# The copy of the transposed product in the delta-rule inverse: from ScalarE to VectorE

## The reference, cut to what matters

```python
m = jnp.where(strict, beta[..., :, None] * kk * decay, 0.0)
a = m + jnp.eye(C, dtype=f32)
...
sol = lax.linalg.triangular_solve(a, rhs, left_side=True, lower=True, unit_diagonal=True)
u, w = sol[..., :DV], sol[..., DV:]
```

## Time and profile before

| | |
|---|---|
| median of 3 runs | 2104.67 us (2101.84 to 2105.86) |
| the profiled execution | 2100.9 us |
| its span, first to last instruction | 2099.0 us |
| granted TensorE clock, mean | 0.961 of full speed |
| TensorE busy | 1930.8 us, 92% |
| VectorE busy | 1279.5 us, 61% |
| ScalarE busy | 984.5 us, 47% |
| the chain that ended last, by engine | PE 85%, DVE 7%, ACT 5%, issue 1%, DMA 1% |

### The profile page before, as it was taken

One profiled execution on the slowest core, in us unless ns is written; L12 is line 12 of the kernel. 1 busy time (PEld: TensorE's weight loads), 2 busy tenths in 40 slices (PEclk: granted clock), 3 DMA queues, 4 the chain that ended last, 5 costly groups with the idle time before them and its releaser, 6 DMA issues.

```text
span 2099.0 us, 27446 instructions
## 1 busy us (share of the span) xinstructions
PE 1930.8 (92%) x10740; PEld 1684.8 (80%) x10740; DVE 1279.5 (61%) x2114; ACT 984.5 (47%) x1629; POOL 82.5 (4%) x160
## 2 busy tenths in 40 slices
PE   6778999889999998999999988689999998978998
PEld 5666888779989896888788877578878887867887
DVE  3635887444443413888798859268878884126664
ACT  3226764345445425765465420265546553026553
POOL 0000001000000000000011100001110010000000
PEclk9899999999999999999999999889999999989999
DMA  4215558432222224657687934268887884424552
GB/s 166 68 51 177 195 195 283 142 112 91 71 101 71 70 76 155 203 190 258 225 305 281 326 130 140 80 221 291 290 294 251 279 310 165 141 74 167 191 190 101
DMA packets 101645, 373.89 MB, mean 178 GB/s; under 512 B 11312, under 2 KB 11472, under 8 KB 101008
## 3 DMA queue, kind: packets, MB, share of 16 engines
q1 hardware_dynamic: 79344, 290.60, 40.2%
q0 software_dynamic: 22176, 81.57, 11.5%
HBM read 371.05 MB, written 1.08 MB: 177 GB/s over the span
## 4 chain that ended last, share of the span: by engine, by line
PE 85%; DVE 7%; ACT 5%; issue 1%; DMA 1%; DVEq 0%; SPq 0%; ACTq 0%
PE ps L402 34%; PE ps L403 18%; PE ps L976 8%; PE ps L351 4%; PE ps L991 3%; PE ps L1704 2%; PE ps L1085 2%; PE ps L1066 2%; PE ps L1080 2%; PE ps L708 2%; PE ps L1581 1%; PE ps L280 1%; DVE arena L1637 1%; DVE weights_lo L390 1%; ACT weights_hi L384 1%
## 5 line engine op out<-in xcount | busy, mean ns | idle before, releaser
L402 PE MATMUL ps<-u_halves,weights_hi 128*128 128x512 f32 x2176 | 765.5, 396 | 21.0 <-DVE u_halves L317 11.8
L403 PE MATMUL ps<-u_halves,weights_lo 128*128 128x256 f32 x2176 | 615.0, 283 | 0.0
L384 ACT ACTIVATE weights_hi<-weight_ring 128x1024 fp32r<-128x1024 f32 x408 | 430.3, 1056 | 363.6 <-PE ps L403 252.9
L390 DVE TENSOR_TENSOR weights_lo<-weight_ring,weights_hi 128x1024 fp32r<-128x1024 f32 x408 | 498.3, 1223 | 152.4 <-ACT weights_hi L384 152.2
L402 PEld LDWEIGHTS ps<-u_halves,weights_hi 128*128 128x128 f32 x2176 | 412.5, 190 | 113.6 <-DVE u_halves L317 13.4
L403 PEld LDWEIGHTS ps<-u_halves,weights_lo 128*128 128x128 f32 x2176 | 417.6, 192 | 0.0
L402 PE MATMUL ps<-act_halves,weights_hi 128*128 128x512 f32 x1088 | 390.9, 403 | 0.0
L403 PE MATMUL ps<-act_halves,weights_lo 128*128 128x256 f32 x1088 | 304.7, 280 | 0.0
L402 PEld LDWEIGHTS ps<-act_halves,weights_hi 128*128 128x128 f32 x1088 | 204.5, 188 | 47.7
L403 PEld LDWEIGHTS ps<-act_halves,weights_lo 128*128 128x128 f32 x1088 | 205.6, 189 | 1.1
L565 DVE SCALAR_TENSOR_TENSOR ffn_tiles<-ffn_tiles,cond 128x1024 f32<-128x1024 f32 x144 | 175.3, 1219 | 0.4 <-DMA ffn_tiles<-in_ada 0.4
(11 more groups left out here) (241 smaller groups left out, 2013.4 us busy)
## 6 DMA issues: line engine op xcount, KB each, us to landing
weight_ring<-in_w SPq DMA_DIRECT2D x545, 512.0 KB, 3.7
ffn_tiles<-in_ada POOLq DMA_DIRECT2D x144, 512.0 KB, 5.1
gdn_tiles<-gates_scratch POOLq DMA_DIRECT2D x8, 512.0 KB, 5.1
consts<-in_consts SPq DMA_DIRECT2D x1, 1664.0 KB, 6.6
arena<-in_alibi POOLq DMA_DIRECT2D x1, 1536.0 KB, 6.6
h<-in_x SPq DMA_DIRECT2D x1, 1024.0 KB, 9.3
out<-u SPq DMA_DIRECT2D x1, 1024.0 KB, 3.9
cond<-in_cond SPq DMA_DIRECT2D x1, 512.0 KB, 7.3
```

The source lines that it names most:

```text
L384: nc.scalar.activation(w_hi[:, m % SPLIT], ring[:, n % RING], ACT.Copy).then_inc(hi_ready, 1)
L390: nc.vector.tensor_tensor(w_lo[:, m % SPLIT], ring[:, n % RING], w_hi[:, m % SPLIT].bitcast(F32), ALU.subtract).then_inc(lo_ready, 1)
L402: nc.tensor.matmul(ps[:, bank], hi, halves, start=start, stop=False, skip_group_check=True)
L403: return nc.tensor.matmul(ps[:, bank, 0:T], lo, halves[:, 0], start=False, stop=stop, skip_group_check=True)
```

## The change

VectorE, no longer ScalarE, copies the transposed product from its bank to `xt_`. The copies keep their size, their semaphores (`g_ix` before, `g_xt` after) and their number. On VectorE both stand behind the two mask products of their doubling and ahead of the taps. ScalarE keeps the copy of X.

```diff
         def level_act(act, i, lv, t):
-            base = 2 * LEVELS * i + 2 * lv + t + 1
             if lv < LEVELS - 1:
                 act.wait_ge(g_xi, 2 * (LEVELS - 1) * i + 2 * lv + t + 1)
                 nc.scalar.activation(flat(x_[:, t]), ps[:, level_bank(lv, "xi", t)], ACT.Copy).then_inc(g_x, 1)
-            act.wait_ge(g_ix, base)
-            nc.scalar.activation(flat(xt_[:, i % 2, t]), ps[:, level_bank(lv, "ix", t)], ACT.Copy).then_inc(g_xt, 1)
...
+        def turned_level_dve(dve, i, lv, t):
+            dve.wait_ge(g_ix, 2 * LEVELS * i + 2 * lv + t + 1)
+            nc.vector.tensor_copy(flat(xt_[:, i % 2, t]), ps[:, level_bank(lv, "ix", t)]).then_inc(g_xt, 1)
+
...
                     level_dve(dve, i, lv, 0)
                     level_dve(dve, i, lv, 1)
+                    turned_level_dve(dve, i, lv, 0)
+                    turned_level_dve(dve, i, lv, 1)
                     if more and lv:
                         for j in fill_tiles(i, lv - 1):
                             taps_conv_dve(dve, steps, i + 1, j)
```

## The result

The changed kernel takes 2144.05 us (median of four runs, 2136.60 to 2145.70), the kernel before 2104.38 us (four runs): ratio 1.0183, 95% interval 1.0156 to 1.0209. The profiled execution took 2142.7 us (span 2140.9). The prediction said 2126 us, at most 2134: right in sign and place, too low by about as much as one of its rivals, the clock, had been priced at.

A forecast was written before the change was run, and what follows sets the result against it. TensorE alone, busy 86.00 of 86.00 us per turn, was taken to set the pace. Nine blocked fill tiles at 2.47 us sum to 22.2 us on the 2104.67 us median, stated as 2126 us, range 2120 to 2134 us.

The forecast's parts named there:

- the clock: Rival: granted clock falls at the nine new TensorE gaps, 9 x 1.92 = 17.3 us on top, 2144 us; chance 0.06.
- The order term: VectorE's taps queue behind copy 1, which waits for the last xt product, delaying fill tiles: 9 x 2.47 = 22.2 us.
- blocked tiles 2, 4 and 7: Fill tiles in doublings 1, 2 and 4 that wait for delayed taps, three per turn with a next one, 2.47 us each.
- release, overlap, taps and restart: Parts of each blocked tile's 2.47 us: release 0.04, copy 0.69 less 0.08 overlap, three taps 1.51, TensorE restart 0.31 us.
- The copies' own price: 48 copies on VectorE at 0.69 us each, adding 33.1 us to its busy time.
- The rival in which they are covered: Copies fit the 1.57 us slack ahead of tile 2, so TensorE never waits: 2104.7 us; chance 0.04.
- the step on the clock: At TensorE's 2.2 us gaps: clock kept after 1.81 us idle, low after 4.40; 2.2 judged much nearer the former.
- a clock fall or two: Part of the range's high end, 2134 us, beside a dearer copy, the backlog and 2 us between runs.
- The backlog on VectorE: Rival: VectorE's table in doubling 4, or mix and decay in doubling 1, delays the next product: about 2130 us; chance 0.08.
- a margin of 0.27 us in the prediction: Doubling 4: table of M ends 6.59 us after the last xt product, next mask product wanted at 6.86 us.

The follow-up runs named there:

- five products in the gap: Changed kernel plus five extra 128x128 TensorE products, adding nothing to the result, in each gap of doublings 1, 2 and 4, turns 0 to 2: 2129.66 us.
- the versions with other gaps: From the kernel before: only tile 0's copy moved to VectorE, 2116.82 us; or VectorE's taps waiting for the last xt product without copying, 2128.06 us.
- tile 0's copy alone: Kernel before with only tile 0's copy moved to VectorE, tile 1's staying on ScalarE: 2116.82 us, ratio 1.0041.
- the wait alone: Kernel before, ScalarE still copying, with VectorE's taps made to wait for their doubling's last xt product: 2128.06 us, run again 2127.4 us.
- half of copy 1: Changed kernel with only two heads of tile 1 copied ahead of the taps, the other two behind them: 2137.00 us, ratio 1.0137.
- tile 1's copy alone: Kernel before with only tile 1's copy moved to VectorE, tile 0's staying on ScalarE: 2143.87 us, ratio 1.0171.
- copy 1 twice: Changed kernel with tile 1's transpose copied twice in a row ahead of the taps: 2154.74 us, ratio 1.0221.

## Why the prediction was wrong

- **The order term was right.** (2104.67 + 22.2 is 2126.9; the stated 2126 drops the 0.9.) Copy 0.69 us expected, 0.691 measured; gap 2.2 us, 2.2 measured; blocked tiles 2, 4 and 7 and no others, nine waits; 22.2 us expected for nine, and 22.2 us measured where the clock held (five products in the gap). The rows for release, overlap, taps and restart carried over from the kernel before without correction, and the versions with other gaps came out at 6.2 and 16.9 us where the same terms gave 6.2 and 16.7.
- **The copies' own price was right**: nothing, if they stand where no one waits behind them. The rival in which they are covered was wrong only because of the wait in front of copy 1; moved down two lines they are covered.
- **What failed is the step on the clock.** The prediction said that 2.2 us "lies between, much nearer to the one that kept it", and gave this rival 0.06. The rows for it were single ones, 1.81 us and 4.40 us, and nothing in them says that what lies between two points is decided by distance. The clock fell at eight of nine gaps, and five products in the gap, which left its length as it was, kept the clock and took 13.4 us away. The rival was right as a mechanism and its price was close: 9 x 1.92 = 17.3 us expected if it came, 13.4 us measured, since each fall cost 1.69 us and one gap was spared. The 1.92 us came from a tile that was already at the low level when it began, and stayed there for 3.8 of its 5.4 us:

```profile
447.34:451.12 3.78, 3.78 (x10) 2.94 (x10) 3.75 (x11) 0.60 (x1) 0.00 (x0) 0.50 0.43 130
```

  The time of that rival, 2144 us, is the measured one, in part by luck: of the 39.7 us between the medians the four turns explain 34 to 36 us.
- The Trainium skill's page "TensorE: Matmul & The Clock Gate" (HAM oscillation) describes a kernel in which PE waits about 3 to 5 us for a transfer at every tile and is throttled each time. Here shorter waits did it, though not each time: the clock fell at 38 of 45 gaps of 1.9 to 3.0 us.
- **The range** held the order term and its bounds but only "a clock fall or two". The nine gaps are equally long, so what one of them sets off is to be expected at most of them (seven and eight here), and the whole price of 17.3 us belonged in the range.
- **The backlog on VectorE did not come**: in the changed kernel the 1.05 us of the earlier trace rows stayed 1.05 us. There the slow tile 7 gave the table of M 1.7 us more room. With five products in the gap, where that tile took 3.72 us, VectorE still stood idle for 0.28 us between the table and the next mask product, in each of the three turns, against a margin of 0.27 us in the prediction:

```profile
523.43 0.69 DVE L1487 TENSOR_TENSOR gdn_tiles<-ps,consts 128x512 f32<-128x512 f32 x1 [0.28 <-PE ps L1066]
```

## What to carry to other kernels

When an operation moves to another engine, price what is queued behind its wait before its own time: here two copies of 0.69 us that cost nothing in one place cost 22 us two lines higher, because they put a product that ends late ahead of taps that a full TensorE waits for. Where TensorE is at 100% and the full clock, ask of every new gap not only how long it is but whether the clock survives it; a gap of 2.2 us was dearer here by two thirds again where the clock fell (1.69 on 2.47 us). And where what sets a rival off lies between two single rows, nearness to one of them is weak evidence: its chance belongs nearer the middle than 0.06, and its full price in the range. That last advice is a judgement from one case.

## What the runs showed of the hardware that was not expected

The granted clock at gaps in which PE stood, in turns otherwise full, counted by the fill tile behind each gap (3.72 us, or 7.17 us for two, if it held):

| PE stands | kernel | clock fell |
|---|---|---|
| 0.4 us | tile 0's copy alone | 0 of 9 |
| 1.1 us | five products in the gap, doublings 1 and 2 | 0 of 6 |
| 0.3 and 0.5 us | the same, doubling 4 | 0 of 3 |
| 1.6 us | the wait alone, two executions | 0 of 18 |
| 1.9 us | half of copy 1 | 6 of 9 |
| 2.2 us | the change, two executions | 15 of 18 |
| 2.2 us | tile 1's copy alone | 5 of 6 |
| 2.9 us | copy 1 twice | 9 of 9 |
| 3.0 us | tile 1's copy alone, doubling 4 | 3 of 3 |

Gaps of equal length in one execution differ, so the moment at which a gap comes counts beside its length; which moment spares it was not tried. The fall came between 0.9 us before PE's restart and 1.4 us after it, so it can come when PE is already at work again. A fall cost 1.58 to 1.70 us at gaps up to 2.2 us, about 1.5 us at 3.0 us, and 1.4 to 2.9 us at 2.9 us.

Two smaller ones. A product that waited for its operand cost TensorE 0.16 to 0.26 us beyond the wait itself: in the doublings the mask ended before the product ahead did, and 0.16 us were lost all the same until the mask was halved. And executions of one kernel differ by up to 16 us (2099.49 to 2115.20 for the kernel before in one set of 17), yet little of it lies in the four turns: with the wait alone they took 368.14 and 368.12 us in two executions, and the change's two executions differ there by 1.55 us, one fall of the clock.
